# Two deep-norm layer norms of a two-block transformer, shifted by the mean of three feature tiles while the output projection still runs, with the embedding-projection weights split in its first half

## The reference

```
for i in range(2):
    h = mixer_a(x, ...) if i == 0 else mixer_b(x, ...)   # attention, ends in  (o * silu(z)) @ w_out
    x = layer_norm(ALPHA * x + h, ln_g[i], ln_b[i])      # over the 1024 features of a token
    gate = sigmoid(x @ ple_w_gate[i])
    x = x + gate * (p[i] @ ple_w_proj[i])                # p[i] is 512 x 256
```

## Time and profile before

| | before |
|---|---|
| median of 3 runs | 2708.68 us (2705.96 to 2709.27) |
| the profiled execution | 2705.9 us, span 2703.8 us, mean granted TensorE clock 0.985 |
| busy share: PE, PEld, DVE, ACT, POOL | 96%, 79%, 50%, 28%, 58% |
| output projection's tile 2 starts, layer 1 | 2315.24 us |
| its last matmul starts, layer 1 | 2348.11 us |
| the gate projection's first matmul, layer 1 | 2368.92 us |

### The profile page before, as it was taken

How to read it: one execution, slowest core, us unless ns; L and a number is a source line. 1 busy time by engine, 2 the same in 40 slices (tenths; PEclk the granted TensorE clock), 3 DMA queues, 4 the chain that set the end, 5 groups by cost and what they waited for, 6 DMA issues and landing times.

```text
span 2703.8 us, 39857 instructions
## 1 busy us (share of the span) xinstructions
PE 2587.7 (96%) x14674; PEld 2125.7 (79%) x14674; DVE 1365.0 (50%) x2054; ACT 752.2 (28%) x1566; POOL 1572.1 (58%) x1668
## 2 busy tenths in 40 slices
PE   5999989999999999999999999999999999899998
PEld 4878978888888886878687877777787787677876
DVE  4863555662662758616433333444444444546754
ACT  3223353111111123245321212222222222233523
POOL 2532224675675665433687777776666665655564
PEclk9999999999999999999999999999999999999999
DMA  6341141332332322111233332432333332223221
GB/s 237 120 153 39 32 156 49 130 128 84 108 126 84 118 86 74 55 47 48 78 93 94 93 94 82 129 110 86 102 93 87 102 90 83 86 69 95 86 94 63
DMA packets 79263, 255.57 MB, mean 95 GB/s; under 512 B 9872, under 2 KB 13712, under 8 KB 78864
## 3 DMA queue, kind: packets, MB, share of 16 engines
q1 hardware_dynamic: 61280, 210.59, 24.2%
q10 hardware_dynamic: 17840, 43.03, 5.1%
HBM read 236.28 MB, written 2.10 MB: 88 GB/s over the span
## 4 chain that ended last, share of the span: by engine, by line
PE 42%; POOL 29%; issue 20%; DVE 5%; DMA 1%; ACT 1%; POOLq 1%; SPq 0%; DVEq 0%; ACTq 0%
POOL w_lo L427 17%; POOL w_hi L425 10%; PE PS L433 8%; PE PS L436 8%; PE PS L434 8%; PE PS L1502 4%; PE PS L1503 4%; PE PS L1504 4%; POOL word L420 2%; PE PS L1489 1%; DVE Z L2224 1%; PE PS L1376 1%; DMA modt<-in_wmod 1%; PE PS L1691 1%; DVE XL L2231 1%
## 5 line engine op out<-in xcount | busy, mean ns | idle before, releaser
L427 POOL TENSOR_TENSOR w_lo<-raw,w_hi 128x512 fp32r<-128x512 f32 (+1 forms) x662 | 953.6, 1441 | 55.3
L433 PE MATMUL PS<-XH,w_hi 128*128 128x512 f32 x2168 | 821.2, 379 | 32.8 <-ACT TH L2152 8.2
L434 PE MATMUL PS<-XL,w_hi 128*128 128x512 f32 x2168 | 792.0, 373 | 0.0
L436 PE MATMUL PS<-XH,w_lo 128*128 128x512 f32 x2168 | 744.0, 374 | 0.0
L420 POOL TENSOR_TENSOR word<-ones 128x1 f32<-128x1 f32 x331 | 94.6, 286 | 1062.4 <-PE PS L436 692.2
L425 POOL TENSOR_SCALAR w_hi<-raw 128x512 fp32r<-128x512 f32 (+1 forms) x662 | 533.5, 806 | 0.0
L433 PEld LDWEIGHTS PS<-XH,w_hi 128*128 128x128 f32 x2168 | 410.4, 189 | 143.0 <-issue 20.5
L434 PEld LDWEIGHTS PS<-XL,w_hi 128*128 128x128 f32 x2168 | 410.4, 189 | 75.0
L436 PEld LDWEIGHTS PS<-XH,w_lo 128*128 128x128 f32 x2168 | 379.4, 189 | 60.0
L1502 PE MATMUL PS<-XH,w_hi 128*128 128x512 f32 (+1 forms) x640 | 236.2, 369 | 10.6 <-DVE XL L2231 10.6
L1503 PE MATMUL PS<-XL,w_hi 128*128 128x512 f32 (+1 forms) x640 | 228.9, 358 | 0.0
(11 more groups left out here) (329 smaller groups left out, 3228.1 us busy)
## 6 DMA issues: line engine op xcount, KB each, us to landing
raw<-in_wgu SPq DMA_DIRECT2D x88, 512.0 KB, 3.5
raw<-in_wa SPq DMA_DIRECT2D x80, 512.0 KB, 3.5
modt<-in_wmod SPq DMA_DIRECT2D x48, 512.0 KB, 10.0
raw<-in_win SPq DMA_DIRECT2D x48, 512.0 KB, 3.6
modv<-in_wmod ACTq DMA_DIRECT2D x48, 512.0 KB, 4.7
raw<-in_wdn SPq DMA_DIRECT2D x32, 512.0 KB, 3.5
QS<-Z ACTq DMA_DIRECT2D x100, 128.0 KB, 3.4
raw<-in_wout SPq DMA_DIRECT2D x16, 512.0 KB, 3.5
```

The lines of the kernel that those rows point to most:

```text
L427: pool.tensor_tensor(lo, src, hi.bitcast(FP32), ALU.subtract).then_inc(s_split, 1)
L433: pe.matmul(acc(s)[:, a:b], hi, rh[:, i, a:b], start=i == 0, stop=False)
L434: pe.matmul(acc(s)[:, a:b], hi, rl[:, i, a:b], start=False, stop=False)
L436: last = pe.matmul(acc(s)[:, a:b], lo, rh[:, i, a:b], start=False, stop=i == k - 1)
```

## The change

With `LN_S = 3`, the layer norm's first moment is taken from feature tiles 0 to 2 alone, during the output projection. VectorE sums those three, TensorE makes their partition sum between tile 3 and tile 4, ScalarE turns it into a provisional mean. Tiles 0 to 2 are shifted by it afterwards; tiles 3 to 7 are prepared as `ALPHA * X2 - mean` ahead of their projection and then get `Z` added. ScalarE squares each shifted tile during the projection, VectorE adds squares 1 to 5 to the first (`SA`) and sums tiles 3 to 5 in `ZS`. VectorE takes tile 7 straight from PSUM. After tile 7 TensorE makes six partition sums: three of shifted tiles (`ZS`, tile 6, tile 7) into bank 7, three of squares (`SA`, squares 6 and 7) into bank 6. From these come the shift's error `DL` and the variance. VectorE centres the tiles a second time by `DL`, the first three before the reciprocal root, the others inside the scaling loop. Then come the products of `p`: three before the gate projection, two between the steps of its first two tiles.

The split of the embedding-projection weights moves: ScalarE makes `PWH` right after it has moved out tile 0, and GpSimd makes `PWL` in two halves, ahead of the weight splits of tiles 2 and 3. SyncE's order of loads is not changed. The waits of the new instructions, the core of the diff:

```diff
-            def ple(l):
-                pool.wait_ge(s_pw, 16 * (l + 1))
-                pool.tensor_scalar(PWH[:], PWR[:], 1.0, 0.0, ALU.mult, ALU.add).then_inc(s_pwh, 1)
-                pool.wait_ge(s_pwh, l + 1)
-                pool.tensor_tensor(PWL[:], PWR[:], PWH[:].bitcast(FP32), ALU.subtract).then_inc(s_pwl, 1)
+            def out_and_ple(s, l):
+                for u in range(KT):
+                    if u in (2, 3):
+                        half = slice((u - 2) * KT, (u - 1) * KT)
+                        pool.wait_ge(s_pwh, l + 1)
+                        pool.tensor_tensor(PWL[:, half], PWR[:, half], PWH[:, half].bitcast(FP32), ALU.subtract).then_inc(s_pwl, 1)
+                    split_weights(pool, s + u)
                 eight(N_PLE[l])
...
                 for u in range(2, KT):
+                    if u == LN_S + 1:
+                        l = done // KT - 2
+                        pe.wait_ge(s_lacc, (LN_S - 1) * (l + 1))
+                        pe.matmul(PS[:, 6, :], ones[:], TH[:, 0:SEQ], start=True, stop=True).then_inc(s_lsum, 1)
                     gemm_tile(pe, s + u, YH2, YL2, SEQ)
...
             def layer_norm(l):
-                p_tile(l, 0)
-                p_tile(l, 1)
-                pe.wait_ge(s_lacc, (KT + 1) * (l + 1))
-                pe.matmul(PS[:, 6, :], ones[:], TH[:, 0:SEQ], start=True, stop=True).then_inc(s_lsum, 1)
-                p_tile(l, 2)
-                for k in range(KT):
-                    pe.wait_ge(s_sq, sums_before(5) + KT * l + k + 1)
-                    pe.matmul(PS[:, 6, :], ones[:], Z[:, k % 4, 0:SEQ], start=k == 0, stop=k == KT - 1).then_inc(s_lsq, 1)
+                pe.wait_ge(s_lda, (KT - LN_S - 3) * (l + 1))
+                pe.matmul(PS[:, 7, :], ones[:], ZS[:], start=True, stop=False)
+                pe.wait_ge(s_used, used(N_PLE[l] - 2))
+                pe.matmul(PS[:, 7, :], ones[:], X2[:, KT - 2], start=False, stop=False)
+                pe.wait_ge(s_lsa, (KT - 3) * (l + 1))
+                pe.matmul(PS[:, 6, :], ones[:], SA[:], start=True, stop=False)
+                pe.wait_ge(s_sq, sums_before(5) + KT * l + KT - 1)
+                pe.matmul(PS[:, 6, :], ones[:], SQL[0][:], start=False, stop=False)
+                pe.wait_ge(s_evac, N_PLE[l])
+                pe.matmul(PS[:, 7, :], ones[:], X2[:, KT - 1], start=False, stop=True).then_inc(s_lds, 1)
+                pe.wait_ge(s_sq, sums_before(5) + KT * (l + 1))
+                pe.matmul(PS[:, 6, :], ones[:], SQL[1][:], start=False, stop=True).then_inc(s_lsq, 1)
+                for u in range(3):
+                    p_tile(l, u)
...
             def ple(l):
-                p_tile(l, 3)
-                p_tile(l, 4)
-                first_tiles(pe, N_PLE[l], XH2, XL2, SEQ, s_xl, KT * (5 + 2 * l))
+
+                def between(i):
+                    if i in (1, 3):
+                        p_tile(l, 3 + i // 2)
+                first_tiles(pe, N_PLE[l], XH2, XL2, SEQ, s_xl, KT * (5 + 2 * l), between=between)
...
                 act.wait_ge(s_used, used(s - 1))
-                for u in range(KT):
-                    if u == 4:
-                        act.wait_ge(s_praw, 16 * (l + 1))
-                        act.activation(PH[:], Praw[:], ACT.Copy).then_inc(s_ph, 1)
+                plain(s, 0)
+                act.wait_ge(s_pw, 16 * (l + 1))
+                act.activation(PWH[:], PWR[:], ACT.Copy).then_inc(s_pwh, 1)
+                plain(s + 1, 0)
+                act.wait_ge(s_praw, 16 * (l + 1))
+                act.activation(PH[:], Praw[:], ACT.Copy).then_inc(s_ph, 1)
+                for u in range(2, LN_S + 1):
                     plain(s + u, 0)
+                act.wait_ge(s_lsum, l + 1)
+                act.activation(TH[:, 0:SEQ], PS[:, 6, :], ACT.Copy, scale=1.0 / (LN_S * P)).then_inc(s_mu, 1)
+                roots()
+                for k in range(LN_S):
+                    act.wait_ge(s_lnd, (KT + LN_S) * l + k + 1)
+                    square(k)
+                for u in range(LN_S + 1, KT - 1):
+                    plain(s + u, 0)
+                    act.wait_ge(s_used, used(s + u - 1))
+                    square(u - 1)
...
+                dve.wait_ge(s_mu, l + 1)
+                prepared(LN_S)
+                shifted(LN_S)
+                for k in range(LN_S):
+                    dve.tensor_tensor(X2[:, k], X2[:, k], mean, ALU.subtract).then_inc(s_lnd, 1)
+                prepared(LN_S + 1)
+                shifted_square(1)
+                shifted_square(2)
+                for u in range(LN_S + 1, KT - 1):
+                    shifted(u)
+                    prepared(u + 1)
+                    shifted_square(u - 1)
+                dve.wait_ge(s_tile, s + KT)
+                dve.tensor_tensor(X2[:, KT - 1], X2[:, KT - 1], acc(s + KT - 1)[:, 0:SEQ], ALU.add).then_inc(s_evac, 1)
...
+                link(dve.scalar_tensor_tensor(out=TH[:, 0:SEQ], in0=DL[:], scalar=-1.0, in1=DL[:], op0=ALU.mult, op1=ALU.mult))
+                dve.wait_ge(s_lsq, l + 1)
+                dve.scalar_tensor_tensor(out=TH[:, 0:SEQ], in0=PS[:, 6, :], scalar=1.0 / D, in1=TH[:, 0:SEQ],
+                                         op0=ALU.mult, op1=ALU.add).then_inc(s_var, 1)
+
+                def centred(k):
+                    dve.tensor_tensor(X2[:, k], X2[:, k], DL[:], ALU.subtract).then_inc(s_lnd, 1)
+                for k in range(3):
+                    centred(k)
...
                 for k in range(1, KT):
                     upper(k)
                     biased_lower(k - 1)
+                    if k + 2 < KT:
+                        centred(k + 2)
```

More of the change, by code:

```diff
@@ L62 @@
 V_BANK = (1, 3, 4, 5, 7, 6, 1, 3)
+LN_S = 3
 B_Q, B_Z = (0, 1, 3, 5, 7, 9, 11, 13), (2, 4, 6, 8, 10, 12, 14, 15)
@@ L511, in build_program @@
         Praw = place("Praw", [P, 2, SEQ], addr=addr_of["X"])
+        SA, DL, SQL0, SQL1 = (place(name, [P, SEQ], addr=addr_of["QK1"] + i * SEQ * 4) for i, name in enumerate(("SA", "DL", "SQL0", "SQL1")))
+        SQL = (SQL0, SQL1)
         s_b2 = sem("second_block_constants_loaded")
@@ L534, in build_program @@
         s_lacc = sem("ln_sums_accumulated")
+        s_lsa = sem("ln_squares_accumulated")
+        s_lda = sem("ln_shifted_accumulated")
+        s_lds = sem("ln_shift_error_summed")
+        s_dl = sem("ln_shift_error_made")
+        s_var = sem("ln_variance_made")
         s_xb = sem("ln_bias_added")
@@ L606, in second_pool @@
                     split_weights(pool, N_A + t, 2 * A_TILES * i)
-            eight(N_AOUT)
-            ple(0)
+            out_and_ple(N_AOUT, 0)
             for t in range(3):
@@ L614, in second_pool @@
                         split_weights(pool, N_BQZ + 8 * kv + u, 4 * i)
-            eight(N_BOUT)
-            ple(1)
+            out_and_ple(N_BOUT, 1)
         def second_pe(pe):
@@ L954, in eight, with square @@
             def eight(s, l):
+                def square(k):
+                    if k >= 3:
+                        act.wait_ge(s_lsa, (KT - 3) * l + k - 2)
+                    act.activation(SQL[k % 2][:] if k else SA[:], X2[:, k], ACT.Square).then_inc(s_sq, 1)
                 act.wait_ge(s_used, used(s - 1))
-                for u in range(KT):
-                    if u == 4:
-                        act.wait_ge(s_praw, 16 * (l + 1))
-                        act.activation(PH[:], Praw[:], ACT.Copy).then_inc(s_ph, 1)
-                    plain(s + u, 0)
+                plain(s, 0)
[5 more added lines that the diff above has]
+                for u in range(2, LN_S + 1):
+                    plain(s + u, 0)
+                act.wait_ge(s_lsum, l + 1)
[8 more added lines that the diff above has]
+                    square(u - 1)
+                act.wait_ge(s_used, used(s + KT - 2))
+                square(KT - 2)
+                act.wait_ge(s_evac, s + KT)
+                square(KT - 1)
             def split_x(q, counted):
@@ L968, in layer_norm @@
             def layer_norm(l):
[L969 to L978, removed]
+                act.wait_ge(s_lds, l + 1)
+                act.activation(DL[:], PS[:, 7, :], ACT.Copy, scale=1.0 / D).then_inc(s_dl, 1)
+                act.wait_ge(s_var, l + 1)
+                rstd(TH[:, 0:SEQ], TH[:, 0:SEQ], 1.0, 1).then_inc(s_rstd, 1)
                 def biased(k):
@@ L1141, in eight, with shifted_square, prepared, shifted @@
             def eight(s, l):
[L1143 to L1147, removed]
+                mean = TH[:, 0:SEQ]
+                def shifted_square(k):
+                    dve.wait_ge(s_sq, sums_before(5) + KT * l + k + 1)
+                    dve.wait_ge(s_lsa, (KT - 3) * l + k - 1)
+                    dve.tensor_tensor(SA[:], SA[:], SQL[k % 2][:], ALU.add).then_inc(s_lsa, 1)
+                def prepared(u):
+                    x = X2[:, u, :]
+                    link(dve.scalar_tensor_tensor(out=x, in0=x, scalar=ALPHA, in1=mean, op0=ALU.mult, op1=ALU.subtract))
+                def shifted(u):
+                    dve.wait_ge(s_evac, s + u + 1)
```

(16 more changed lines are left out.)

10 lines of the change are left out of this document (8 added, 2 removed).

## The result

| | before | after |
|---|---|---|
| median | 2709.27 us (2705.96 to 2714.38, 5 runs) | 2723.56 us (2717.99 to 2728.24, 5 runs) |
| profiled execution: span, mean clock | 2703.8 us, 0.985 | 2721.8 us, 0.979 |

The ratio is 1.0047, with a 95% interval of 1.0034 to 1.0060: the changed kernel is slower. The medians differ by 14.3 us, and the ratio makes 12.7 us of 2709.27. 2719 was forecast, 10.3 over the median then shown. One of the 23 runs of before beside e10 and e11 took 5100 us, and the ratios leave it out as slow.

A forecast was written before the change was run, and what follows sets the result against it. The prediction took TensorE, busy for 96% of the span, as the bound, with GpSimd's weight splits almost as long. Per layer 11.0 + 0.9 - 6.3 = 5.6 us late, 11.2 in all, gave 2719 us, range 2711 to 2729.

The forecast's parts named there:

- Term 1: Ahead of out tile 2: TensorE waits for `PWR`'s landing, copy, half `PWL` and split; tile 3 starts 11.0 us late.
- The clock: In out tile 2: after almost 11 us idle TensorE runs at clock 0.50, costing 2.2 us, 0.7 at tile 3.
- Term 2: Between out tiles 3 and 4: the added partition sum on TensorE makes the projection 0.9 us late.
- Term 3: During out tiles 4 to 7: VectorE's and ScalarE's new operations put nothing on the path; tile 7 finds VectorE idle.
- Term 4: From the end of tile 7 to the end of the gate pair: 25.9 us against 32.2, 6.3 us earlier.
- The cover: Ahead of out tile 2: copy and half `PWL` are done when tile 0 ends, giving 2698 us; chance 0.08.
- The rival by port: From the mean to tile 6's end: VectorE blocks GpSimd's splits, tile 7 8.4 us later, 2736 us; chance 0.07.

The follow-up runs named there:

- e10: e9 with three idle matmuls around the last steps of out tiles 0 and 1; median 2704.88 us, ratio 0.9975 to the kernel before.
- e11: The kernel before with three idle matmuls around the last steps of out tiles 0 and 1; median 2709.18 us, ratio 0.9989.
- e4: The changed kernel with the halves of `PWL` ahead of tiles 3 and 4 instead of 2 and 3; median 2711.05 us, ratio 1.0000 to before.
- e9: The changed kernel with VectorE instead of GpSimd making `PWL`, in halves; median 2705.59 us, ratio 0.9987 to the kernel before.
- e12: The kernel before with three idle matmuls, `PWH` made early by ScalarE and `PWL` in halves by VectorE; median 2705.33 us, ratio 0.9987.
- e2: The kernel before (old layer norm) with only the weight split moved early as in the change; median 2724.65 us, ratio 1.0041.
- e1: The changed kernel with `PWH` and `PWL` both made by GpSimd after its eighth tile, as before; median 2715.98 us, ratio 1.0012 to before.
- e8: The kernel before once more, unchanged, one profile; in its second layer tile 2 took 7.6 us.
- e5: The changed kernel with ten idle matmuls of 0.87 us ahead of out tile 2; median 2722.10 us, ratio 1.0047 to the kernel before.
- e3: The changed kernel with `PWL` made whole by GpSimd after its eighth split, `PWH` still early on ScalarE; median 2712.60 us, ratio 1.0007 to before.
- e6: The changed kernel without the second centring by `DL`, one profile; tail after tile 7 25.1 us in layer 1, 27.4 in layer 2.

## Why the prediction was right

**Term 1** was right in each step. Landing after 6.2 us (6.3 forecast), copy 1.91 (1.9), half of `PWL` 2.35 (2.45), first half of the split 2.9 (2.75), tile 2 8.8 late (8.8), tile 3 11.0 and 11.2 late (11.0). Undoing the order confirms the cause: with the halves one tile later or elsewhere, tile 2 starts 4.6 to 5.2 us after the issue (e4, e9, e10, e12), and with the old layer norm the stall stands unchanged (e2, 13.5 and 13.6).

**The clock** was right in level and in its price for tile 2: 0.50 stands over the first 4.7 us of tile 2, up to 2329, and the tile takes 7.8 us instead of 5.64. Two things were wrong. First, the forecast tied the fall to the long stall alone, and it also comes earlier. In layer 1 the clock was already down in 2312 to 2315, after the wait of 2.18 us for `YL`; it was back at 1.00 in 2316 to 2318 and fell again in the stall, to 0.50 from 2320 on. In layer 2 it fell once, within 2 us of the issue, and stayed down. In kernels without the long stall it falls after the short wait too, in some executions (e1, e9, layer 2 of e4 and of e8). Second, "only 0.7 us hang on the clock" was too little at tile 3: the first half of its split was ready 19.8 us after the issue, not 20.6 as forecast, and TensorE came at 21.2, so the clock held tile 3 by some 1.4 us. In e9 and e8 the same drop lengthens tile 2 by 1.5 to 2 us. What this is worth at the end of the layer is another matter: in e5 an earlier tile 3 brought nothing.

**Term 2**, 0.9 late: the lateness grows from 11.0 to 11.9 between tiles 3 and 7.

**Term 3**: nothing on TensorE's path, but not for the reason given. The forecast gave VectorE's 19 operations 20.1 us (8, 4.4, 4.4 and three of 1.1); without a pause they took 23.2 (2339.28 to 2362.48), and tile 7 did not find it idle. Beside VectorE's new operations GpSimd needs 6.05 us per tile (its tiny instruction starts at 2344.26, 2350.34 and 2356.39) instead of 4.5; VectorE's scalings and additions take up to 1.78 us instead of 0.7. GpSimd is slower there than TensorE's 5.5 us per tile, as is VectorE in tile 5 (5.6 us from one addition of `Z` to the next), and only the lead that they had at tile 4 covers three tiles. It is used up at the end: the third sum waits 0.29 us for `SA`. In e1 and e3 the lead is gone, and the price is the whole gain.

**Term 4**, 6.3 earlier: 6.1 and 6.3. The first gate matmul came at 11.5 (11.1) and the pair took 14.65 (14.8), two small misses that cancel. The attribution was wrong. The prediction priced the old split of `PWH` and `PWL` at the 1.33 us wait that it left; it cost 3.1 (e2, e12), since it also pushed GpSimd's gate splits under the centring. About half of the gain is the split's (32.2 to 29.1, e2) and half the norm's (29.1 to 26.1). Two terms that I costed apart are one.

**The rivals.** The cover did not hold: GpSimd waited. The rival by port had its mechanism right and its place wrong: the strong form of the exclusion is shown by 4.97, 5.04 and 5.00 us for a 0.7 us operation behind a long GpSimd one. This agrees with what the Trainium skill states (SBUF — State Buffer, "Who interferes with whom"). Against GpSimd's short splits less is lost: 1.5 us more per tile, where full exclusion by four operations of 0.68 us would be 2.7, and this rival had 12.9 us over 2.5 tiles. Tile 7 was not late by it.

**The size.** Per layer 5.8 was measured against 5.6. The median moved by 14.3 instead of 10.3, and the interval of the ratio, 9.2 to 16.3 us, contains the forecast. The layers' 11.6 us stand against the ratio's 12.7. That the forecast median of 2719 is 4.6 us short of the measured one is within the scatter of the runs and no sign for or against a term. In the profiled pair, 6.2 us more lie in the attention stretch, which no term had. What makes it 197.7 in one trace and 204.4 in another is open: a wait of 3.4 us for the scalings occurs in six of the 14 traces, in stretches of 203.9 and 204.4 but also of 200.3 to 201.6 (e4, e5, e6, e11). No run tested it.

## What to carry to other kernels

Before an instruction is put in front of a queue's steady work, look up when its input is issued, not only how long it takes: here one loop index decided between 1.0047 and 1.0000. A long GpSimd operation costs what VectorE wanted to do in that time. Ask whose chain that is, and price a moved operation by the kernel without it, not by the wait it left behind. Give such work to the engine that has the lead, and time each part of a change alone and together. An engine that keeps pace only by a lead is the next limit: freeing TensorE ahead of it (e5) brought nothing.

## What the runs showed of the hardware

- ScalarE's copy of 128x2048 from fp32 to fp32r takes 1.91 us and GpSimd's 1.91, 2.35 beside VectorE (e1). The remainder of 128x1024 took GpSimd 2.35 to 3.38 (e4) and VectorE 1.21 to 2.32.
- TensorE's granted clock fell to 0.50 after waits as short as 2.2 us, even after 8.7 us of back-to-back matmuls against ones (e5). It does not do so in every execution: of the twelve profiled layers without the long stall and without idle matmuls, six had it down at some time between the wait for `YL` and the end of tile 2 (both of e1 and e9, one each of e4 and e8), and six had not. With three idle matmuls in that wait and the next it stayed at 1.00 in all six layers (e10, e11, e12).
- A VectorE operation of 0.7 us took 4.97 to 5.04 us when it began 0.4 to 0.6 us behind a GpSimd subtraction of 4.9 to 5.1 us (e1, e3). Between streams of short operations GpSimd's split went from 4.5 to 6.05 us and VectorE's operations to as much as 1.78 us.
